# Convolution units shared with VectorE, one hand-written list for the selection, and closer steps for the gated unit and swish

## The reference, cut to what matters

```python
h = rms_norm(x, norm_g) @ w_in            # 7748 columns, cut into the parts below
# A: for each query the best 256 keys by an index score, then attention over them
_, sel = lax.top_k(score, topk)
# B: gated unit over chunks of 128 positions
v = layer_norm(v); out_b = u * (W_s @ v + b)
# C: GLU, causal depthwise convolution of 31 taps, layer norm, swish
c = a * sigmoid(g); y = conv(c, w, 31 taps) + b; out_c = silu(layer_norm(y))
# each branch gated, multiplied by its matrix, summed; then a second small block
```

## Time and profile before

| | us |
|---|---|
| median of three runs | 2918.38 |
| profiled execution | 2916.02 |
| its span, first to last instruction | 2914.2 |
| TensorE busy in the span | 2697.1 |
| VectorE busy | 1962.8 |
| ScalarE busy | 1503.0 |
| GpSimd busy | 1315.7 |

### The profile page before, as it was taken

One profiled execution on the slowest core, in us unless ns is written; L12 is line 12 of the kernel. 1 busy time (PEld: TensorE's weight loads), 2 busy tenths in 40 slices (PEclk: granted clock), 3 DMA queues, 4 the chain that ended last, 5 costly groups with the idle time before them and its releaser, 6 DMA issues. The chain is left out here.

```text
span 2914.2 us, 40267 instructions
## 1 busy us (share of the span) xinstructions
PE 2697.1 (93%) x14029; PEld 2488.9 (85%) x14029; DVE 1962.8 (67%) x4027; ACT 1503.0 (52%) x2633; POOL 1315.7 (45%) x939
## 2 busy tenths in 40 slices
PE   6999999899999897948999878899999999999998
PEld 6999999899999897848999756777788998888886
DVE  6477769979896866550463378889976667555554
ACT  5376698788778676735312267677760002111111
POOL 1100387789798666629545354321244332111110
PEclk9999999999999998979999989999999999999999
DMA  4433223333332223212465543221136556121121
GB/s 164 124 124 133 92 82 119 105 121 114 112 121 93 93 73 102 89 59 91 154 195 171 158 123 93 68 59 51 51 117 243 165 167 228 48 71 57 62 71 37
DMA packets 271865, 320.43 MB, mean 110 GB/s; under 512 B 37041, under 2 KB 235185, under 8 KB 271021
## 3 DMA queue, kind: packets, MB, share of 16 engines
q1 hardware_dynamic: 171123, 190.02, 21.2%
q10 hardware_dynamic: 100538, 127.82, 12.4%
HBM read 196.36 MB, written 120.73 MB: 109 GB/s over the span
## 5 line engine op out<-in xcount | busy, mean ns | idle before, releaser
L1640 PE MATMUL psum<-hT_hi,j_whi 128*128 128x416 f32 x2440 | 876.5, 359 | 90.5 <-POOL j_wlo L1449 60.4
L1640 PE MATMUL psum<-hT_hi,j_wlo 128*128 128x416 f32 x2440 | 862.6, 354 | 0.0
L1640 PE MATMUL psum<-hT_lo,j_whi 128*128 128x416 f32 x2440 | 861.5, 353 | 0.0
L1255 POOL TENSOR_TENSOR v_y<-v_y,v_product 128x422 f32<-128x422 f32 x540 | 615.6, 1180 | 43.1 <-ACT v_product L1237 42.9
L1640 PEld LDWEIGHTS psum<-hT_hi,j_whi 128*128 128x128 f32 x2440 | 463.6, 190 | 102.4 <-issue 66.0
L1640 PEld LDWEIGHTS psum<-hT_lo,j_whi 128*128 128x128 f32 x2440 | 464.6, 190 | 9.6 <-issue 1.6
L448 DVE TENSOR_SCALAR_CACHE_REDUCE s_tie<-s_key,s_bits 128x640 bf16<-128x640 f32 (+14 forms) x352 | 464.2, 1319 | 12.3
L1640 PEld LDWEIGHTS psum<-hT_hi,j_wlo 128*128 128x128 f32 x2440 | 462.9, 190 | 6.0
L1237 ACT ACTIVATE v_product<-v_x,v_taps 128x422 f32<-128x422 f32 x600 | 351.7, 639 | 192.4 <-POOL v_y L1255 177.8
L1449 POOL TENSOR_TENSOR j_wlo<-j_w,j_whi 128x1024 fp32r<-128x1024 f32 x61 | 151.3, 2480 | 275.4 <-ACT j_whi L1484 275.3
L1502 ACT ACTIVATE j_out<-psum 128x416 f32<-128x416 f32 x285 | 143.7, 505 | 248.6 <-PE psum L1640 236.2
(11 more groups left out here) (293 smaller groups left out, 4856.4 us busy)
## 6 DMA issues: line engine op xcount, KB each, us to landing
T_dram<-j_out ACTq DMA_DIRECT2D x59, 624.0 KB, 2.9
j_w<-in_w_in ACTq DMA_DIRECT2D x59, 512.0 KB
m_gate<-T_dram SPq DMA_DIRECT2D x60, 416.0 KB, 3.5
T_dram<-j_out ACTq DMA_DIRECT2D x59, 416.0 KB, 2.4
m_oraw<-B_dram SPq DMA_DIRECT2D x15, 832.0 KB, 5.6
M_dram<-m_merged ACTq DMA_DIRECT2D x5, 1664.0 KB, 7.5
n_x<-in_x_prompt SPq DMA_DIRECT2D x16, 512.0 KB, 5.3
f_mraw<-M_dram SPq DMA_DIRECT2D x16, 512.0 KB, 4.6
```

Source lines behind the costliest of these rows:

```text
L1255: pool.tensor_tensor(y[k % 2][:], y[k % 2][:], product[n % RING][:], ALU.add).then_inc(added, 1)
L1640: last = pe.matmul(bank, w[p][:, k, :], h[:, k, t0:t0 + SPAN], start=(k == 0 and q == 0), stop=(k == KD - 1 and q == 2))
```

## The change

Three of the twenty convolution units (piece 2 of slots 0, 1 and 2) move to VectorE, which does them in the middle of the selection: one multiply, one `tensor_scalar`, thirty `scalar_tensor_tensor`, each waiting for the one before. The other 17 stay on ScalarE and GpSimd, over 42 jobs. The computed plan of the selection becomes the literal list `PLAN`, with the time of each entry's end in us from the start of the selection; the order of the tiles stays. ScalarE's step loses the instruction that wrote `a_value`: the next one reads the integer copy. Its count and sign move to PSUM bank 7. The cost of a step in the account falls from 1.25 to 1.0 us beside the scores. The gated unit starts at job 54, span 2, with steps of 12 slices; swish has steps of 20.

```diff
-UNITS = 4 * len(CONV_SPANS)
+OWN = [(0, 2), (1, 2), (2, 2)]
+SHARED = [(s, x) for s in range(4) for x in range(len(CONV_SPANS)) if (s, x) not in OWN]
+UNITS = len(SHARED)
-CONV_FROM, CONV_JOBS = 9, 43
-GMLP_FROM = (50, 4)
+CONV_FROM, CONV_JOBS = 9, 42
+GMLP_FROM = (54, 2)
-def select_times(): ...
-ACT_DUE, FINISHED = select_times()
+PLAN = [("offer", 9, 3), ("unit", 0, 24), ("whole", 4, 75), ("offer", 12, 79), ("unit", 1, 100), ("complete", 9, 146), ("whole", 5, 202),
+        ("offer", 13, 206), ("complete", 12, 263), ("whole", 6, 325), ("offer", 14, 329), ("complete", 13, 386), ("whole", 7, 453),
+        ("offer", 15, 457), ("complete", 14, 517), ("whole", DT, 586), ("offer", 11, 589), ("complete", 15, 653), ("whole", 2, 693),
+        ("offer", 10, 697), ("complete", 11, 747), ("whole", 3, 793), ("offer", 8, 796), ("complete", 10, 847), ("unit", 2, 868),
+        ("complete", 8, 932)]
+ACT_DUE = [us + 10 + 0.02 * us for what, _, us in PLAN if what == "offer"]
+    a_cnt, a_turn = c.psum[:, 7, 0:1], c.psum[:, 7, 1:2]
+        def move_own(i):
+            s, x = OWN[i]
+            sp.wait_ge(own_done, i + 1)
+            sp.dma_start(c.Y_dram[s, :, x * CW_SPAN:(x + 1) * CW_SPAN], own_y[:, 0:CW_SPAN]).then_inc(own_moved, 16)
-        for t, us in FINISHED:
+        for what, t, us in PLAN:
+            if what == "offer":
+                continue
             units(SELECT_US + us)
-            if t == FINISHED[-1][0]:
+            if what == "unit":
+                move_own(t)
+                if t + 1 < len(OWN):
+                    load_own(t + 1)
+                continue
-            return keys_of(ACT_TILES[self.turn]) * 0.00084 + 1.25
+            return keys_of(ACT_TILES[self.turn]) * 0.00084 + 1.0
-                self.steps.did(act.activation(a_value[:], a_turn[:], ACT.Identity, scale=2.0 ** (b + 15), bias=value))
+        def unit(i):
+            s = OWN[i][0]
+            tap = lambda k: c.parT[:, s, k:k + 1]
+            if i == 0:
+                c.wait_for_parameters(vec)
+            vec.wait_ge(own_full, 32 * (i + 1))
+            do(vec.tensor_tensor(own_x[:], own_x[:], own_y[:], ALU.mult))
+            y = own_y[:, 0:CW_SPAN]
+            do(vec.tensor_scalar(y, own_x[:, 0:CW_SPAN], tap(0), tap(CONV), ALU.mult, ALU.add))
+            for k in range(1, CONV):
+                ins = vec.scalar_tensor_tensor(out=y, in0=own_x[:, k:k + CW_SPAN], scalar=tap(k), in1=y, op0=ALU.mult, op1=ALU.add)
+                if k < CONV - 1:
+                    do(ins)
+            ins.then_inc(own_done, 1)
 # gated unit
-    STEP, TURN_AT, MIX_AT = 20, (0, 10), (5, 15)
+    STEP, TURN_AT, MIX_AT = 12, (0, 6), (3, 9)
-        if (d, k) == (2, 12):
+        if (d, k) == (2, 8):
 # swish
-    STEP, SQUARES, SPREAD = 28, 15, 27
+    STEP, SQUARES, SPREAD = 20, 15, 27
```

More of the change, by code:

```diff
@@ L277 @@
 LIFT = 1
-ACT_TILES = [9, 12, 13, 14, 15, 11, 10, 8]
-DVE_TILES = [4, 5, 6, 7, DT, 2, 3]
-LOADED = [(9, 0), (4, 1), (12, 2), (5, 1), (13, 0), (6, 1), (14, 2), (7, 1), (15, 0), (DT, 1), (11, 2), (2, 1), (10, 0), (3, 1), (8, 2)]
[L283 to L307, removed]
-ACT_DUE, FINISHED = select_times()
+PLAN = [("offer", 9, 3), ("unit", 0, 24), ("whole", 4, 75), ("offer", 12, 79), ("unit", 1, 100), ("complete", 9, 146), ("whole", 5, 202),
[3 more added lines that the diff above has]
+        ("complete", 8, 932)]
+ACT_TILES = [t for what, t, _ in PLAN if what == "offer"]
+ACT_DUE = [us + 10 + 0.02 * us for what, _, us in PLAN if what == "offer"]
+LOADED = [(9, 0), (4, 1), (12, 2), (5, 1), (13, 0), (6, 1), (14, 2), (7, 1), (15, 0), (DT, 1), (11, 2), (2, 1), (10, 0), (3, 1), (8, 2)]
 KEYS = 3
@@ L339, in stage_select @@
     bits, flip = (sb(f"s_{n}", [P, 1], I32) for n in ("bits", "flip"))
-    a_cnt, a_turn, a_value, a_first, a_start = (sb(f"s_a{n}", [P, 1]) for n in ("cnt", "turn", "value", "first", "start"))
-    a_bits = sb("s_abits", [P, 1], I32)
+    a_first, a_start, a_bits = sb("s_afirst", [P, 1]), sb("s_astart", [P, 1]), sb("s_abits", [P, 1], I32)
+    a_cnt, a_turn = c.psum[:, 7, 0:1], c.psum[:, 7, 1:2]
     a_found, a_mask = ([sb(f"s_a{n}{k}", [P, 1], I32) for k in range(2)] for n in ("found", "mask"))
@@ L344, in stage_select @@
     a_least = sb("s_aleast", [P, 2])
+    own_x, own_y = sb("s_ownx", [P, CW_SPAN + LEFT]), sb("s_owny", [P, CW_SPAN + LEFT])
     c.after_select = sb.at
     S = c.sem
+    own_full, own_done, own_moved = S("s_own_full"), S("s_own_done"), S("s_own_moved")
     own_steps, act_steps = S("s_steps"), S("s_act_steps")
@@ L378, in units, with load_own @@
                 upcoming[0] += 1
+        def load_own(i):
+            s, x = OWN[i]
+            if i:
+                sp.wait_ge(own_moved, 16 * i)
+            c.wait_for_stored(sp, 4 + 2 * s)
+            first = x * CW_SPAN - LEFT
+            for buf, slot in ((own_x, S_GA), (own_y, S_GG)):
+                sp.dma_start(buf[:], c.T_dram[slot + s, :, first:first + CW_SPAN + LEFT]).then_inc(own_full, 16)
+        def move_own(i):
+            s, x = OWN[i]
+            sp.wait_ge(own_done, i + 1)
+            sp.dma_start(c.Y_dram[s, :, x * CW_SPAN:(x + 1) * CW_SPAN], own_y[:, 0:CW_SPAN]).then_inc(own_moved, 16)
         for t, _ in LOADED[:KEYS]:
             load(t)
+        load_own(0)
         for t in range(2):
@@ L385, in sync @@
         waiting = LOADED[KEYS:]
-        for t, us in FINISHED:
+        for what, t, us in PLAN:
+            if what == "offer":
+                continue
             units(SELECT_US + us)
-            if t == FINISHED[-1][0]:
+            if what == "unit":
[3 more added lines that the diff above has]
+                continue
+            if t == PLAN[-1][1]:
                 for k in range(KEYS):
@@ L425, in step @@
             tops = key[slot[t]][:].bitcast(BF16)[:, 1:2 * n:2]
-            level, value = (a_bits[:].bitcast(F32), a_value[:]) if b < 14 else (a_first[:], a_start[:])
+            level, value = (a_bits[:].bitcast(F32), a_bits[:]) if b < 14 else (a_first[:], a_start[:])
             if b == 14:
@@ L505, in vector @@
         without_search(1)
[L506 to L513, removed]
+        for what, t, _ in PLAN:
+            if what == "offer":
+                offer(ACT_TILES.index(t))
+            elif what == "complete":
+                complete(ACT_TILES.index(t))
+            elif what == "whole":
+                whole(t)
+            else:
+                unit(t)
     def wait_for_selected(eng):
         eng.wait_ge(early_stored, 32)
+        eng.wait_ge(own_moved, 16 * len(OWN))
         for k in range(KEYS):
@@ L1172, in load @@
     def load(sp, u):
-        s, x = u // 5, u % 5
+        s, x = SHARED[u]
         if u == 0:
@@ L1286, in stage_convolve @@
     c.load_unit, c.move_unit = load, move
+    c.wait_for_parameters = lambda eng: eng.wait_ge(par_ready, 2)
     c.wait_for_moved = lambda eng: eng.wait_ge(unit_moved, UNITS)
```

8 lines of the change are left out of this document (4 added, 4 removed).

## The result

| | before | after |
|---|---|---|
| median of the compared runs, us | 2917.99 (2917.39 to 2918.76) | 2836.22 (2834.72 to 2843.17) |
| profiled execution, us | 2916.02 | 2835.52 |
| its span, us | 2914.2 | 2833.7 |
| mean granted TensorE clock | 0.968 | 0.982 |

The ratio is 0.9724, with a 95% interval of 0.9707 to 0.9741: 82 us faster. Forecast were 2826 us, with a range of 2800 to 2868.

A forecast was written before the change was run, and what follows sets the result against it. It took 117 us of TensorE time as lost in the selection, from a queue order on times VectorE does not keep. Gain 100, less 6 (tail) and 2 (end), is 92: 2916.0 to 2824, median 2826 us; range 2800 to 2868.

The forecast's parts named there:

- (1): Selection: the new list, ending at 932 us, removes the queue's stall chain; last tile done near 1215 to 1240 us.
- (2): Selection, 17 shared units over 42 jobs: per 150 us, ScalarE falls from 129 to 121 us, GpSimd from 122.5 to 108.
- (3): ScalarE's search step: 0.3 us shorter, 36 us less in all; off the path, only shortens VectorE's waits.
- (4): VectorE's three convolution units: 22, 45 and 45 us, bounds 22 and 58; 6 us of stall charged at unit 1.
- the 8 us for keys and values: Selection, job 18: first load waits behind tile 13's search burst; a stall of 5 us and slow clock of 3 remain.
- (5): Tail, gated unit in closer steps: 5 us lost, between no stall and 15 us.
- (6): Tail, swish in closer steps: late pieces cost 14 us; with the gated unit's 5, net tail loss taken as 6.
- (7): End of projection: the barrier before attention waits for swish's last store, 2 us lost, between 0 and 8.
- D: Rival, whole kernel: all stalls go and the tail costs nothing more, 2801 us; chance 0.09.
- B: Rival, tail: packing binds, gated unit costs 15 us in place of 5, swish 24 more, 2860 us; chance 0.13.
- C: Rival, selection: everybody waits for VectorE, third unit ends near 1328 us; slower, about 2958 us; chance 0.06.
- A: Rival, selection: ScalarE's bursts still stall TensorE through late evacuations, 2861 us; chance 0.14.

The follow-up runs named there:

- e9: The kernel before with only the new list's times for the tiles, which also shift ScalarE's search due times: 2805.49 us, ratio 0.9625.
- e10: The kernel before with only the new search step and its account at 1.0, old computed times kept: 2816.49 us, ratio 0.9668.
- e8: The changed kernel with the running sum of VectorE's convolution units in PSUM, only the last tap writing to SBUF: 2834.87 us, ratio 0.9721.
- e3: The changed kernel with no units on VectorE, all 20 shared by ScalarE and GpSimd over 42 jobs: 2836.39 us, ratio 0.9726.
- e4: The changed kernel with the old search step (fourth instruction back, count and sign in SBUF), account still 1.0: 2845.83 us, ratio 0.9759.
- e1: The changed kernel with the old tail (gated unit from job 50, steps of 20 slices; swish steps of 28): 2804.86 us, ratio 0.9620.
- e7: The changed kernel without GpSimd's multiply of u by z in the gated unit, that product left out: 2819.17 us, ratio 0.9667.
- e11: The changed kernel with the old tail and the running sum of VectorE's units in PSUM: 2802.92 us, ratio 0.9618.

## Why the prediction was right, and where not

The forecast was 10 us too low (2826 for 2836.2). The gain in the selection was 9 us larger than its 100, the loss in the tail 22 us larger than its 8 (jobs 50 to 60 took 325.4 us in place of 299.1, and the barrier 4.1 more). So it is right in kind and in its large term, and the small term is mis-sized. That it came out this near is in part luck, since the two errors have opposite signs: with the loss in the tail alone it would have been some 2845 us, above the 2842 up to which the forecast was to hold.

- **What bounds the kernel.** Right: 117 us were lost in the selection, and the order of the queue is what made GpSimd and then TensorE late, for 87 of the 101.5 us that TensorE waited there. The trace of before shows the chain four times, and e9 takes it away: other times in the list, and 110 us are gone. What part of these is the queue's times and what part the due times stays open.
- **(1) The new list.** Right in its time: the last tile was stored at 1235 us, predicted 1215 to 1240. GpSimd's wait on the queue is gone. What it missed is that the old order was also a loop, which a faster search step breaks as well (e10). It treated the list as necessary; it is sufficient, and the step with its account nearly so.
- **(2) Fewer units on ScalarE and GpSimd.** ScalarE came to 116.7 us of 150, predicted 121 and then 116 with the step. GpSimd came to 128.8, predicted 108. 6.5 us of that are VectorE's unit 1, beside which its additions are longer (122.3 in e8). For the rest, these 150 us hold 85 additions where they held 90, so 5 fewer and not 12, and even in e8 they take 1.22 us in place of 1.13, with VectorE busy for 141 us of the 150 in place of 107. Over 350 to 1350 us the relief is there, 739 us of GpSimd and 700 of ScalarE against 814 and 753 in e3, but it was not needed.
- **(3) The search step.** Its size was right: 0.31 us for 0.3. "Off the path and only shortens VectorE's waits" was wrong. By itself it is worth 99 us (e10), and on top of the list and the units still 10 (e4). In e4, though, the account stayed at 1.0 while the step was 0.3 us longer again; e9, whose account is the old 1.25 and whose units are all shared, loses nothing against e1. e4's loss lies beside and behind unit 1, where (4) charged 6 us for the meeting of unit and burst. Whether the account or the unit makes the difference to e9 was not tried.
- **(4) VectorE's units.** 23.1, 39.9 and 38.7 us, predicted 22, 45 and 45, within the bounds of 22 and 58. What the Trainium skill says in "SBUF — State Buffer", "Who interferes with whom", is what happens, and e8 shows it. The middle value was nearer than the 58 us, since a third of the taps met no hold and the others waited 0.8 us in the mean, not a whole addition. The stall of 6 us at unit 1 did not come: 797 matmuls stand from 350 to 500 us. With the 8 us for keys and values (5.1 and 0.8 of waits, and the clock behind them) and 3 for other bursts, 17 us were kept back and about 8 were lost: 109 gained for 100.
- **(5) The gated unit: the step that was mis-sized.** Predicted a loss of 5 us, at most 15; it was 24. Jobs 50 to 57 took 230.7 us in place of 210.7, and the 210.7 had 4.4 us of swish's matmuls in them, which come later now. Nearly all of it is in jobs 55 to 57, the three stretches below. At full rate they are 67.8 us and their 204 inserted matmuls 23.5, at 0.115 us for one in job 53 of before; they took 115.7:

```profile
1374.10:1413.40 39.30, 33.90 (x206) 32.64 (x204) 30.05 (x64) 8.13 (x14) 13.25 (x6) 0.96 0.59 186
1413.40:1451.40 38.00, 33.41 (x194) 32.40 (x194) 31.20 (x60) 6.64 (x11) 17.97 (x8) 0.91 0.66 211
1451.40:1489.80 38.40, 31.76 (x170) 30.29 (x169) 19.67 (x46) 4.92 (x7) 18.30 (x10) 0.91 0.48 151
```

VectorE is busy for 61.25 us in the first two, which hold 6.7 steps of 12 slices: 9.2 us for each, of 9.5 that a step has at full rate (6.8 and 2.75 for the inserts). On top it must wait in its own order for TensorE's mixing, and TensorE for it. The prediction had the 20.3 of 19.1 us in its hand, for two pairs, and took part of them as waits that would shrink ("its own part being near 13"). Its own part was about right: with each operation at its shortest length the nine pairs have 53 us of work, 12 for two pairs. The other 37 of VectorE's 90 us were operations held by GpSimd (37 of 89 before), which stay as long as GpSimd's multiplies stay, and they are counted as busy. e7 shows the share: without one of GpSimd's multiplies per pair 17 us go. The other part of the miss is the clock: 0.91 in two of three stretches, on top of the waits that a row shows (13.7 + 2.9 us).
- **(6) Swish.** Right in the main. Jobs 58 to 60 took 94.6 us in place of 88.4, and 4.4 of the difference are matmuls of swish that used to lie in jobs 56 and 57: 2 us lost, predicted 0. The squares of piece 2 were late by 4.0 us, predicted 2 or 5: the text does not say whether its 3 us of slow clock are in the 5 or on top, and its sum of 14 comes out only with them on top. They are the longest wait of the swish, but not of the tail: the gated unit has one of 4.6.
- **(7) The end.** The barrier's wait went from 4.4 to 8.5 us: 4 lost for 2. Of e1's 31 us, then, about 24 are the gated unit's, 2 swish's and 4 the barrier's.
- **Rivals.** D's 2801 us was out of reach because of the tail, and e1 and e11, which lack the new tail, came within 4 us of it. B was right about the gated unit and wrong about swish: its price for the gated unit, 15 us, was too low, that for swish, 24, far too high. C never came near: the third unit was done at 1176 us. A's evacuation waits did not come.

## What to carry to other kernels

Before work is moved to another engine to relieve two, look whether the stall is a matter of order. Here a queue that obeys planned times was behind its plan, and correcting the times alone gave the whole gain; the moved units added nothing to it (by themselves, under the old times, they were not run). If an engine's operations can be held by another's, its busy time has the holds in it, and they do not shrink when its steps are packed closer: here VectorE had 9.2 us of work for steps of 9.5, and 24 us were lost. A change with two halves is measured by halves: this one had about -109 and +31 us in it, and the version with the good half alone wins.

## What was not expected of the hardware

- An operation of four columns can take 2.3 us in place of 0.16, the whole length of GpSimd's operation beside it. It also holds for a `tensor_scalar` with one tensor input: the gated unit's L740 (128x512) takes 535 ns at least and 2739 at most. 9 of its 17 are held in the changed kernel and 7 in the one before (L722 there), which moves the median from 547 to 2587 ns but the mean only from 1.42 to 1.66 us. The section of the Trainium skill named above has `tensor_scalar` among the operations that can take the ports shared with GpSimd; these lengths agree.
- With the sum in PSUM the same taps are not held at all (87 of them between 661 and 665 ns) and take as long as with it in SBUF undisturbed (660), though each reads and writes PSUM.
- Small ScalarE operations (128x1) are 295 ns with operands in SBUF, 236 with input and output in PSUM and 262 with the input alone there. Reading the accumulator falls from 188 to 152 ns when it goes to PSUM.
